# Two modulation pieces of a two-layer block, computed between the layers instead of inside the second layer's attention

## The chip, the cores and the metric

The kernel runs on one core of one Trainium2 chip. The metric is the device time of one execution in microseconds (us). TensorE is called PE below (its weight loads PEld), VectorE DVE, ScalarE ACT, and SP is the engine whose queue issues nearly all transfers from HBM.

## The reference, cut to what matters

```python
# first block: two layers (l = 0, 1) over an x stream and a context stream y, 256 rows of 1024 each
for l in range(2):
    shift, scale, gate       = split(silu(c)     @ w_mod[l] + b_mod[l], 3)   # 3 x 1024, for x
    shift_c, scale_c, gate_c = split(silu(c_ctx) @ w_mod[l] + b_mod[l], 3)   # 3 x 1024, for y
    hx = rmsnorm(x, norm_g[l]) * (1 + scale)   + shift
    hy = rmsnorm(y, norm_g[l]) * (1 + scale_c) + shift_c
    f, g, q, k, v, a = branches(h @ w_in[l], ...)        # Fourier, gated and attention branch
    ox = attend(qx, [ky; kx], [vy; vx]) * silu(ax)       # 8 heads, 256 queries, 512 keys
    x  = x + gate * (concat(fx, gx, ox) @ w_out[l])
    if l == 0:
        y = y + gate_c * (concat(fy, gy, oy) @ w_out[l])
# second block: dilated attention, convolution, gates, layer norms and a feed-forward part on x
```

Everything is float32. The product `silu(c) @ w_mod[l]` has 3072 columns per layer. The kernel computes it in six pieces of 512 columns: pieces 0 and 1 are the shift, 2 and 3 the scale, 4 and 5 the gate. A gate piece is needed only when the output projection `w_out` of its layer is added to x.

## The kernel before, in words

Four engine programs are written out by hand, one function per engine (`tensor_program`, `scalar_program`, `vector_program`, `sync_program`), and run each in its own order; semaphores join them. There is no scheduler.

**Weights.** A weight chunk is up to 128 x 1024 floats (512 KB). SP loads it into one of four raw slots (`NRAW = 4`, line 2101). ACT copies it into a rounded high part `whi` (line 960), DVE subtracts to get the low part `wlo` (line 1417), and PE multiplies three times per 128 x 128 block: high by high, high by low, low by high (lines 362, 363, 365 and 367 in `lin`, 379 to 392 in the halves `lin_first` and `lin_rest`, 409 to 415 in `lin_many`). There are five slots of high and low parts (`NHL = 5`). ACT prepares up to four chunks ahead of the one that PE uses and DVE up to three; `Weights.ahead` stops such looking ahead at a chunk that is not split. SP issues in the order in which PE takes chunks, and waits for each until the raw slot four chunks back is free: for a split chunk when DVE has made its low part, for an unsplit one when PE has read it.

**Modulation pieces.** One piece is four groups (`mod_g`, line 464). A group is one 512 KB chunk of `w_mod` and two matmuls of 128 x 32 by 128 x 512, which appear as four instructions; successive matmuls write to three different 32-row strips of one PSUM bank. After the fourth group ACT copies the bank to `modrow` (`row`, line 964), PE turns it with four transposes (`mod_t`, line 482), and DVE sums and adds the bias (`bias`, lines 1446 and 1449). Pieces of layer 0 and pieces 0 to 3 of layer 1 are computed in layer 0, with weights in places of their own. Pieces 4 and 5 of layer 1 (the gate) go through the raw slots as unsplit chunks and are computed in the second layer's attention: `mod_order(MODS1)` gives ten steps, group by group with two transposes between them, and items 0 to 9 take one each (the call `mod_step` in `for i in range(ni + 4)`).

**Attention.** An item is one head and one block of 128 queries. In item i PE does the scores of i (line 700), the transposes of i - 3 (708), the modulation step, every second item the values (723), and through item 7 one half of a gate projection `agate` (379 to 392). DVE takes the maximum (1759), ACT the exponential (1187), DVE the scaling (1766, 1768), ACT copies the transposes (1194).

**Between the layers.** PE ends layer 0 with the eight column blocks of `w_out`, then sums squares for the row norm with tiny matmuls (774 for what has been added up by DVE, 777 for the last block), DVE computes the reciprocal root (1458 to 1462), PE spreads it over the partitions (501), DVE and ACT make `hh` and `hl` of layer 1 column block by column block (1470, 983, 1480), and PE begins `lin_many`: five projections at once, as the blocks appear. Then come `lin_tm` (432 to 440), the sums 580 and 584, two transposes (592), the key, value and query projections (599, 601, 609), the Fourier branch (640, 650, 664, 665), three projections, and the transposes of the heads (619), which DVE (1682) and ACT (1114) copy out.

**PSUM.** Eight banks are handed out by `Psum.take`: of the banks not held, the one whose last use began longest ago.

Of the kernel before, what the change touches and what calls it, by code (L numbers as in the profile page):

```python
# [14 lines left out]
P = 128  # L15
# [12 lines left out]
NEG = -1.0e30  # L28
WTOTAL = 128 * (248320 - 40 * 1024)

# [174 lines left out]
def geometry(K):  # L205

    G = []
    for l in range(2):
        g = State()
        o = 0  # L210

        def area(n):
            nonlocal o
            a = K.AF[:, o:o + n]
            o += n
            return a
# [71 lines left out]

MODS0 = ((0, 4), (0, 5), (1, 2), (1, 3), (1, 0), (1, 1))
MODS1 = ((1, 4), (1, 5))  # L290


def mod_order(jobs):

    out = []
    for i, a in enumerate(jobs):
        out.append(("g", a, 0))
        if i:
            out.append(("t", jobs[i - 1], 0))
        out += [("g", a, g) for g in (1, 2, 3)]  # L300
    out.append(("t", jobs[-1], 0))
    return out

# [37 lines left out]
def tensor_program(K, e):  # L341
# [102 lines left out]
    def mod_g(l, n, g):  # L444

        key = ("mod", l, n)
        if g == 0:
            pe.wait_ge(*ps.take(key, hold=True))
        pe.wait_ge(A["c32"])
        early = l == 0 and n in EARLY  # L450
        c = None
        if early:
            pe.wait_ge(K.m_in[4 * EARLY.index(n) + g]["in"])
            w = K.early(4 * EARLY.index(n) + g).rearrange("p (k n) -> p k n", k=2)
        elif (l, n) in MODS0:
            pe.wait_ge(K.mw_in[g]["in", MODS0.index((l, n))])
            w = K.mslot(g)
        else:
            c, w, _ = weights((*key, g), ("w_mod", l, (2 * g, 2 * g + 1), (512 * n, 512)), 1024, split=False)
            w = w.rearrange("p (k n) -> p k n", k=2)  # L460
# [5 lines left out]
        if c is not None:  # L466
            W.given[c] = M.now()
        if g == 3:
            ps.drop(key)

    def mod_piece(q):

        for g in range(4):
            mod_g(*MODS0[q], g)
        if q:
            mod_t(*MODS0[q - 1])

    def mod_t(l, n):
# [4 lines left out]
        i.then_inc(*M.up(key))  # L483

    def mod_step(what, a, g):
        if what == "g":
            mod_g(*a, g)
        else:
            mod_t(*a)

# [58 lines left out]
    def layer(l):  # L549
# [181 lines left out]
        mt = lambda k: V[l, "mix", k]  # L731
        steps = mod_order(MODS1) if l else []
        half = None
        for i in range(ni + 4):
# [27 lines left out]
            if i >= ni:  # L762
                begun.append(lin_first((l, "wout", i - ni), "w_out", l, (P * (i - ni), P), 4, xh, xl, N, mt))
        for s in steps:
            mod_step(*s)
# [13 lines left out]

    layer(0)  # L780
    spread(("h", 1), TT)
    ps.drop(("h", 1, "b"))
    layer(1)


# [162 lines left out]
def scalar_program(K, e):  # L948
# [17 lines left out]

    def mod_step(what, a, g, prev):
        if what == "g":
            highs(("mod", *a, g))
            if g == 3:  # L970
                row(*a, prev)

    def square(key, src, z, n, *after):
# [44 lines left out]
    def mod_row(q):  # L1018
        row(*MODS0[q], MODS0[q - 1] if q else (0, 1))

    def layer(l):
# [179 lines left out]
        ni = len(items)  # L1201
        steps, prev = mod_order(MODS1) if l else [], (1, 1)
        for i in range(ni + 4):
# [18 lines left out]
            if l == 0 and i == 16:  # L1222
                heads_T("q", 1, 0, 1, M[l, "s", 15])
            if steps:
                s = steps.pop(0)
                mod_step(*s, prev)
                if s[0] == "g" and s[2] == 3:
                    prev = s[1]
            if i in BESIDE[l] and BESIDE[l][i][0] != "gws":
# [7 lines left out]
            if i >= ni:  # L1237
                highs((l, "wout", i - ni), 4 - i + ni)
        for s in steps:
            mod_step(*s, prev)  # L1240
            if s[0] == "g" and s[2] == 3:
                prev = s[1]

        for m in range(KD):
# [9 lines left out]
    highs((1, "fin", 1), 0)  # L1254
    ac.wait_ge(M[0, "wout", 7])
    for k in range(KD):
        make_h(1, k)
# [147 lines left out]
def vector_program(K, e):  # L1405
# [122 lines left out]
    def layer(l):  # L1528
# [26 lines left out]
        V.mark((l, "tab"))  # L1555
        if l == 0:
            bias(0, 4)

# [220 lines left out]

        ni = len(items)  # L1780
        steps = mod_order(MODS1) if l else []

        def mod_step(what, a, g_):
            if what == "t":
                bias(*a)
            else:
                lows(("mod", *a, g_))

        for i in range(ni + 4):
# [6 lines left out]
            if l == 0:  # L1796
# [26 lines left out]
                if i == 16:  # L1823
                    heads_T("q", 1, 0, 1, M[l, "s", 15])
            if steps:
                mod_step(*steps.pop(0))
            if 0 <= i - 4 and items[i - 4][1] == 7:
# [11 lines left out]
            if i >= ni:  # L1839
                lows((l, "wout", i - ni), min(3, 4 - i + ni))  # L1840
        for s in steps:
            mod_step(*s)
        for k in range(4, 8):
# [239 lines left out]
def sync_program(K, e):  # L2083
# [20 lines left out]
    def mods(q):  # L2104

        for g in range(4):
            sp.wait_ge(K.mm[("mod", *MODS0[q - 1])] if q else K.mm["mod", 0, 1])
            e.dma_start(K.mslot(g), K.wmod[16 + 4 * q + g].rearrange("p (k n) -> p k n", k=2)).then_inc(*K.mw_in[g].up(("in", q)))

# [16 lines left out]
    mods(5)  # L2126
    chunks(19, len(W.plan))
    for t in range(2):
# [6 lines left out]
def build(nc, cpack, xin, wpack, wmod, wuq, wukv, l2rows, out):  # L2135
    with ExitStack() as ctx:
# [47 lines left out]

        def mslot(g):

            G = K.G[0]
            return (G.ag[:, 0:2, :], G.ag[:, 2:4, :], G.ug, G.Pb.rearrange("p (a n) -> p a n", a=4)[:, 0:4:3, :])[g]

# [8 lines left out]
        K.m_in = [sig(f"mod_in{i}", 16) for i in range(16)]  # L2198
        K.mw_in = [sig(f"modw_in{i}", 16) for i in range(4)]
        K.c0, K.c1, K.c2, K.uq_in, K.ukv_in, K.l2_in, K.s_out = (sig(n, 16) for n in ("c0_in", "c1_in", "c2_in", "uq_in", "ukv_in", "l2_in", "out_done"))  # L2200
# [155 lines left out]
```

## Time and profile before

| what | us |
|---|---|
| median of 3 runs | 941.96 |
| lowest and highest run | 941.86, 943.33 |
| the profiled execution, its time | 940.3 |
| its span, first to last instruction | 938.5 |
| PE busy in the span | 878.3 |
| DVE busy | 615.4 |
| ACT busy | 427.1 |

The profiled execution took 1.8 us more than its span. The page gives busy times, the chain of work that ended last and the costliest groups; the timeline gives single instructions in order of time, with the idle time before them and its releaser in brackets; PEclk is the clock that TensorE was granted, 1.00 for 2.4 GHz and 0.50 for 1.2 GHz. The passage between the layers lies at about 293 to 304 us, the rest of the second layer before its attention at 304 to 378 us, and items 0 to 9 of the second layer's attention at 378 to 418 us.

### The profile page before, as it was taken

What the parts mean: (1) busy time and instruction counts of PE and PEld (TensorE: products, weight loads), DVE (VectorE), ACT (ScalarE), POOL (GpSimd) and SP (SyncE); (2) the same over time, 40 slices, a digit from 0 to 9 for tenths busy, and PEclk for the clock granted to TensorE, in tenths of its full rate; (3) what the DMA queues carried; (4) which work ended last, traced back from release to release, by engine and by line L of the source; (5) the groups of instructions that cost most, each with busy time, mean ns of one, the idle gap of its engine ahead of it and who ended that gap; (6) DMA issues with size and microseconds to landing.
All of it is one profiled execution on the core that took longest, in us unless ns stands there. A gap on an engine that the chain in (4) does not pass through costs nothing.

```text
span 938.5 us, 13733 instructions
## 1 busy us (share of the span) xinstructions
PE 878.3 (94%) x5592; PEld 724.6 (77%) x5592; DVE 615.4 (66%) x1212; ACT 427.1 (46%) x710; POOL 0.2 (0%) x4
## 2 busy tenths in 40 slices
PE   4899999999997999999999999798989799999996
PEld 1568468767685868567998888788889699999995
DVE  4432848574756579456699999986677745544555
ACT  3342426443533463555534454465543654444441
POOL 0000000000000000000000000000000000000000
PEclk9899999999998999999999999999999899999998
DMA  9674542100322213533455664442346265556551
GB/s 359 244 297 169 202 179 78 46 1 19 118 68 84 85 44 131 176 105 135 160 186 175 202 221 141 129 132 58 126 136 209 83 193 174 175 200 199 178 163 45
DMA packets 39999, 136.71 MB, mean 146 GB/s; under 512 B 4352, under 2 KB 4480, under 8 KB 39680
## 3 DMA queue, kind: packets, MB, share of 16 engines
q1 hardware_dynamic: 38928, 130.48, 41.0%
q10 hardware_dynamic: 1008, 5.36, 1.4%
q8 instruction: 44, 0.72, 0.3%
q14 instruction: 19, 0.16, 0.0%
HBM read 134.77 MB, written 1.05 MB: 145 GB/s over the span
## 4 chain that ended last, share of the span: by engine, by line
PE 80%; DVE 14%; ACT 3%; DMA 1%; issue 1%; SPq 0%; DVEq 0%; ACTq 0%
PE ps L362 9%; PE ps L363 9%; PE ps L367 8%; PE ps L922 6%; PE ps L432 3%; PE ps L434 3%; PE ps L433 3%; PE ps L464 3%; PE ps L700 3%; DVE wlo L1417 2%; DVE AF L1888 2%; PE ps L390 2%; PE ps L723 2%; PE ps L609 2%; PE ps L391 1%; PE ps L392 1%
## 5 line engine op out<-in xcount | busy, mean ns | idle before, releaser
L1417 DVE TENSOR_TENSOR wlo<-raw,whi 128x1024 fp32r<-128x1024 f32 (+2 forms) x204 | 233.8, 1161 | 59.6 <-ACT whi L960 59.4
L960 ACT ACTIVATE whi<-raw 128x1024 fp32r<-128x1024 f32 (+2 forms) x204 | 204.0, 1005 | 116.4 <-DMA raw<-wpack 51.2
L362 PE MATMUL ps<-hh,whi 128*128 128x256 f32 (+1 forms) x736 | 216.8, 295 | 3.7 <-DVE AF L1933 2.6
L363 PE MATMUL ps<-hl,whi 128*128 128x256 f32 (+1 forms) x736 | 213.1, 290 | 0.0
L367 PE MATMUL ps<-hh,wlo 128*128 128x256 f32 (+1 forms) x640 | 185.3, 289 | 0.0
L362 PEld LDWEIGHTS ps<-hh,whi 128*128 128x128 f32 x736 | 141.5, 192 | 9.7 <-issue 5.1
L363 PEld LDWEIGHTS ps<-hl,whi 128*128 128x128 f32 x736 | 141.7, 192 | 3.0 <-issue 0.7
L367 PEld LDWEIGHTS ps<-hh,wlo 128*128 128x128 f32 x640 | 123.0, 192 | 1.4
L432 PE MATMUL ps<-whi,hh 128*128 128x512 f32 (+1 forms) x192 | 70.8, 369 | 0.8 <-ACT wk L1063 0.8
L433 PE MATMUL ps<-wlo,hh 128*128 128x512 f32 (+1 forms) x192 | 70.2, 366 | 0.0
L434 PE MATMUL ps<-whi,hl 128*128 128x512 f32 (+1 forms) x192 | 70.2, 366 | 0.0
L2058 DVE TENSOR_TENSOR AF<-AF,ps 128x256 f32<-128x256 f32 x22 | 9.2, 420 | 68.7 <-PE ps L365 68.1
L1888 DVE SCALAR_TENSOR_TENSOR AF<-AF,cst 128x256 f32<-128x256 f32 x120 | 52.0, 485 | 0.4
L1759 DVE TENSOR_REDUCE AF<-ps 128x1 f32<-128x512 f32 (+1 forms) x48 | 28.7, 597 | 30.4 <-PE ps L700 30.4
L1187 ACT ACTIVATE AF<-ps,AF 128x512 f32<-128x512 f32 (+1 forms) x48 | 29.5, 615 | 33.2 <-DVE AF L1759 32.8
L700 PE MATMUL ps<-AF 96*128 96x512 f32 (+1 forms) x96 | 43.5, 535 | 0.9 <-ACT AF L1114 0.9
L1194 ACT ACTIVATE AF<-ps 128x512 f32<-128x512 f32 (+1 forms) x48 | 25.1, 523 | 38.0 <-PE ps L708 37.6
L432 PEld LDWEIGHTS ps<-whi,hh 128*128 128x128 f32 x192 | 36.0, 188 | 6.5 <-DVE wlo L1417 1.0
L464 PE MATMUL ps<-AF,c 128*32 128x512 f32 x160 | 30.1, 618 | 11.5 <-DMA AF<-wmod 11.5
L434 PEld LDWEIGHTS ps<-whi,hl 128*128 128x128 f32 x192 | 36.0, 188 | 5.6
L433 PEld LDWEIGHTS ps<-wlo,hh 128*128 128x128 f32 x192 | 36.1, 188 | 5.4
L708 PEld LDWEIGHTS ps<-cst,AF 128*128 128x128 f32 x160 | 20.2, 141 | 18.9 <-issue 13.8
(268 smaller groups left out, 1554.0 us busy)
## 6 DMA issues: line engine op xcount, KB each, us to landing
raw<-wpack SPq DMA_DIRECT2D x186, 512.0 KB, 4.2
AF<-wmod SPq DMA_DIRECT2D x40, 512.0 KB, 6.4
raw<-wpack SPq DMA_DIRECT2D x24, 256.0 KB, 3.4
XT<-xin SPq DMA_DIRECT2D x4, 512.0 KB, 5.7
raw<-wpack SPq DMA_DIRECT2D x4, 432.0 KB, 5.4
uq<-wuq ACTq DMA_DIRECT2D x2, 768.0 KB, 5.5
cst<-cpack ACTq DMA_DIRECT2D x1, 1093.0 KB, 7.9
AF<-wukv ACTq DMA_DIRECT2D x2, 512.0 KB, 6.8
```

The lines of the kernel that those rows point to most:

```text
L362: e.matmul(o, wh[:, b], xh(k), start=j == 0, stop=False, skip_group_check=True)
L363: e.matmul(o, wh[:, b], xl(k), start=False, stop=False, skip_group_check=True)
L367: e.matmul(o, wl[:, b], xh(k), start=False, stop=False, skip_group_check=True)
L432: e.matmul(o, xh(k)[:, ts], wh[:, b], start=k == 0, stop=False, skip_group_check=True)
L433: e.matmul(o, xh(k)[:, ts], wl[:, b], start=False, stop=False, skip_group_check=True)
L434: i = e.matmul(o, xl(k)[:, ts], wh[:, b], start=False, stop=k == KD - 1, skip_group_check=True)
L464: i = e.matmul(o, K.c32[:, 32 * k:32 * k + 32], w[:, j, :], start=k < 3, stop=k > 4, skip_group_check=True)
L700: e.matmul(ps.ap(key, n), g.Q[0:96, t % 2, h, :], g.K[0:96, h, 0:n], start=True, stop=True, skip_group_check=True).then_inc(*M.up(key))
L922: i = e.matmul(ps.ap(("fd", t), 512, 512 * q), y[:, f % 8, x], w[:, 512 * q:512 * q + 512], start=f == 0 and y is K.fh and w is wh, stop=f ...
L960: e.activation(W.hi(i), W.raw(i), ACT.Copy).then_inc(*HI.up(j))
L1417: e.tensor_tensor(W.lo(i), W.raw(i), W.hi(i), ALU.subtract).then_inc(*LO.up(j))
L1888: e.scalar_tensor_tensor(out=g.CV[:, m, :], in0=g.U[:, m, j:j + 256], scalar=w, in1=g.CV[:, m, :], op0=ALU.mult, op1=ALU.add).then_inc(*V. ...
```

## The change

The list `MODS` now holds pieces (1, 4) and (1, 5) as its seventh and eighth; `mod_order`, `MODS1` and the modulation steps of the attention loops are gone from PE, ACT and DVE. The weights of the two pieces no longer pass through the raw slots: `K.G[0].late`, the last 8192 columns of layer 0's area (its queries, probabilities and keys), takes them, 1024 columns a group, with four more semaphores. SP issues these eight transfers after the chunk of the last `w_out` block of layer 0, once the values of item 30 of layer 0 are done.

PE computes groups 0 and 1 of piece 4 before the sums of squares, groups 2 and 3 after them, groups 0 and 1 of piece 5 after the spreading, groups 2 and 3 after `lin_many`, followed by the transposes of piece 4; the transposes of piece 5 come after the sums of `lin_tm`. ACT copies the row of piece 4 before it makes `hh`, and the row of piece 5 after `fin(1)`. DVE adds the bias of piece 4 after the rotation tables, and that of piece 5 after the statistics.

```diff
-WTOTAL = 128 * (248320 - 40 * 1024)
+WTOTAL = 128 * (248320 - 48 * 1024)
+        g.late = K.AF[:, end - 8192:end]
-MODS0 = ((0, 4), (0, 5), (1, 2), (1, 3), (1, 0), (1, 1))
-MODS1 = ((1, 4), (1, 5))
...
+MODS = ((0, 4), (0, 5), (1, 2), (1, 3), (1, 0), (1, 1), (1, 4), (1, 5))
@@ tensor_program, mod_g
-        elif (l, n) in MODS0:
...
-            c, w, _ = weights((*key, g), ("w_mod", l, (2 * g, 2 * g + 1), (512 * n, 512)), 1024, split=False)
+            q = MODS.index((l, n))
+            pe.wait_ge(K.mw_in[g + 4 * (q == 7)]["in", q])
+            w = K.mslot(q, g)
@@ tensor_program, layer
             lin_many([spec("cq", 0), spec("cq", 1), spec("ckv", 0, True), spec("fin", 0), spec("fin", 1)], ht)
+            mod_g(1, 5, 2)
+            mod_g(1, 5, 3)
+            mod_t(1, 4)
...
         if l == 1:
+            mod_t(1, 5)
...
-            if steps:
-                mod_step(*steps.pop(0))
...
         if l == 0:
+            mod_g(1, 4, 0)
+            mod_g(1, 4, 1)
             key = ("h", 1, "s")
...
     layer(0)
+    mod_g(1, 4, 2)
+    mod_g(1, 4, 3)
     spread(("h", 1), TT)
     ps.drop(("h", 1, "b"))
+    mod_g(1, 5, 0)
+    mod_g(1, 5, 1)
     layer(1)
@@ scalar_program
-            mod_row(1)
+        mod_row(1 if l == 0 else 7)
...
     ac.wait_ge(M[0, "wout", 7])
+    mod_row(6)
@@ vector_program
-        if l == 0:
-            bias(0, 4)
+        bias(l, 4)
...
         V.mark((l, "stat"))
+        if l:
+            bias(1, 5)
@@ sync_program
-            sp.wait_ge(K.mm[("mod", *MODS0[q - 1])] if q else K.mm["mod", 0, 1])
...
+            sp.wait_ge(K.mm[("mod", *MODS[q - 1])] if 0 < q < 6 else K.mm["mod", 0, 1] if q == 0 else K.mm[0, "pv", 30])
...
-    chunks(19, len(W.plan))
+    at_out = W.of[0, "wout", 7] + 1
+    chunks(19, at_out)
+    mods(6)
+    mods(7)
+    chunks(at_out, len(W.plan))
```

PE at the passage between the layers, from the last matmul of layer 0's `w_out` to the first of `lin_many`, before. Here `128x1` rows are the sums of squares, `ps<-wk,cst` is the spreading, and four matmuls are `x4`:

```order
L365 MATMUL ps<-hh,wlo 128x512
L774 MATMUL ps<-cst,acc 128x1 x4
L777 MATMUL ps<-cst,wk 128x1 x4
L501 MATMUL ps<-wk,cst 128x512
L409 MATMUL ps<-hh,whi 128x256
```

The same place in the changed kernel:

```order
L353 MATMUL ps<-hh,wlo 128x512
L448 MATMUL ps<-AF,c32 32x512 x4
L751 MATMUL ps<-cst,acc 128x1 x4
L754 MATMUL ps<-cst,wk 128x1 x4
L448 MATMUL ps<-AF,c32 32x512 x4
L477 MATMUL ps<-wk,cst 128x512
L448 MATMUL ps<-AF,c32 32x512 x4
L397 MATMUL ps<-hh,whi 128x256
```

Three pairs of groups (`32x512 x4`, two groups each) stand between the steps of the passage; the fourth pair stands after `lin_many`.

DVE in the second layer, from the last low part before the head copies to these copies (`1682` before, `1648` now), before. `wlo` rows are low parts, `rtab` rows the rotation of the keys:

```order
L1417 TENSOR_TENSOR wlo<-raw,whi 128x1024
L1656 TENSOR_TENSOR AF<-AF 128x1536
L1637 SCALAR_TENSOR_TENSOR AF<-AF,ps 128x256
L1670 TENSOR_TENSOR AF<-AF,rtab 128x256
...
L1676 TENSOR_TENSOR AF<-AF 128x8x32
L1619 TENSOR_TENSOR AF<-AF,ps 128x256
L1637 SCALAR_TENSOR_TENSOR AF<-AF,ps 128x256
L1682 TENSOR_SCALAR AF<-ps,cst 96x4x128 x2
```

The same place in the changed kernel:

```order
L1382 TENSOR_TENSOR wlo<-raw,whi 128x1024
L1622 TENSOR_TENSOR AF<-AF 128x1536
L1603 SCALAR_TENSOR_TENSOR AF<-AF,ps 128x256
L1382 TENSOR_TENSOR wlo<-raw,whi 128x1024
L1636 TENSOR_TENSOR AF<-AF,rtab 128x256
...
L1642 TENSOR_TENSOR AF<-AF 128x8x32
L1585 TENSOR_TENSOR AF<-AF,ps 128x256
L1382 TENSOR_TENSOR wlo<-raw,whi 128x1024
L1603 SCALAR_TENSOR_TENSOR AF<-AF,ps 128x256
L1648 TENSOR_SCALAR AF<-ps,cst 96x4x128 x2
```

Two low parts, those of the gate projections `agate` 1 and 2, have moved from the attention to the stretch before the head copies, since no unsplit chunk stops the looking ahead there any more. On ACT three high parts (`agate` 1 to 3) have moved in the same way.

## Rows read from the trace of the kernel before

**Rows 1.** The chain that ended last, by engine, on the page.

```profile
PE 80%; DVE 14%; ACT 3%; DMA 1%; issue 1%; SPq 0%; DVEq 0%; ACTq 0%
```

**Rows 2.** Windows: stretch, length, busy PE, PEld, DVE, ACT, POOL, PEclk, DMA share, GB/s.

```profile
378.00:418.00 40.00, 38.06 (x240) 23.46 (x241) 19.25 (x41) 19.63 (x41) 0.00 (x0) 1.00 0.49 164
...
230.00:258.00 28.00, 25.88 (x206) 18.81 (x202) 18.74 (x37) 15.60 (x33) 0.00 (x0) 1.00 0.32 114
```

**Rows 3.** Timeline of PE in the second layer's attention: start, length, line, operation.

```profile
378.15 1.10 PE L700 MATMUL ps<-AF 96*128 96x512 f32 x2 [0.86 <-ACT AF L1114]
...
382.64 1.05 PE L464 MATMUL ps<-raw,c 128*32 128x512 f32 x4
383.62 0.39 PE L390 MATMUL ps<-hh,whi 128*128 128x256 f32 x1
...
397.75 0.50 PE L482 MATMUL ps<-cst,modrow 96*128 96x96 f32 x4
399.46 1.09 PE L723 MATMUL ps<-AF 128*64 128x128 f32 x16 [1.22 <-DVE AF L1637]
...
415.46 0.55 PE L482 MATMUL ps<-cst,modrow 96*128 96x96 f32 x4 [0.57 <-ACT modrow L964]
...
418.51 1.02 PE L700 MATMUL ps<-AF 96*128 96x512 f32 x2
```

**Rows 4.** Waits in 378 to 418 us: total, times, longest.

```profile
DVE wlo L1417 <- ACT whi L960: 16.9, 5, 5.0
...
ACT whi L960 <- DMA raw<-wpack: 8.0, 3, 3.1
```

**Rows 5.** Timeline of PE at the passage and after `lin_many`.

```profile
293.63 0.95 PE L774 MATMUL ps<-cst,acc 128*128 128x1 f32 x8
295.42 1.05 PE L777 MATMUL ps<-cst,wk 128*128 128x1 f32 x8 [0.84 <-ACT wk L976]
298.84 2.08 PE L501 MATMUL ps<-wk,cst 128*128 128x512 f32 x2 [2.37 <-DVE wk L1462]
303.55 0.55 PE L409 MATMUL ps<-hh,whi 128*128 128x256 f32 x1 [2.63 <-DVE hl L1480]
...
323.56 0.37 PE L432 MATMUL ps<-whi,hh 128*128 128x288 f32 x1 [0.85 <-ACT wk L1063]
```

**Rows 6.** Timeline of PE in the first layer: groups of a piece in a row, and a spreading.

```profile
15.66 1.90 PE L464 MATMUL ps<-AF,c 128*32 128x512 f32 x8
18.10 1.13 PE L501 MATMUL ps<-wk,cst 128*128 128x512 f32 x2 [0.53 <-DVE wk L1462]
...
104.84 2.77 PE L464 MATMUL ps<-AF,c 128*32 128x512 f32 x16
```

**Rows 7.** Windows at which the granted clock falls and rises, `lin_many`, and an early load.

```profile
297.00:298.00 1.00, 0.00 (x0) 0.00 (x0) 0.83 (x6) 0.00 (x0) 0.00 (x0) 0.81 0.00 0
307.00:308.00 1.00, 1.00 (x7) 1.00 (x7) 1.00 (x3) 0.65 (x2) 0.00 (x0) 0.57 0.00 0
304.00:321.00 17.00, 17.00 (x110) 15.93 (x110) 10.21 (x25) 5.41 (x12) 0.00 (x0) 0.89 0.01 1
50.00:60.00 10.00, 9.15 (x42) 5.90 (x43) 5.91 (x13) 7.04 (x16) 0.00 (x0) 1.00 0.87 324
```

**Rows 8.** Timeline of DVE before the attention.

```profile
343.68 0.75 DVE L1614 TENSOR_SCALAR AF<-ps,AF 128x512 f32<-128x512 f32 x1 [0.76 <-PE ps L601]
...
366.52 1.22 DVE L1417 TENSOR_TENSOR wlo<-raw,whi 128x1024 fp32r<-128x1024 f32 x1
...
373.24 4.39 DVE L1682 TENSOR_SCALAR AF<-ps,cst 96x512 f32<-96x512 f32 x6
```

**Rows 9.** Timeline: PE's last values of layer 0; ACT's high part of layer 1's first chunk.

```profile
257.11 1.09 PE L723 MATMUL ps<-AF 128*64 128x128 f32 x16
...
274.84 1.05 ACT L960 ACTIVATE whi<-raw 128x1024 fp32r<-128x1024 f32 x1
```

**Rows 10.** One line of DVE: the sum over a turned piece.

```profile
L1446 DVE TENSOR_REDUCE mod<-ps x12: 172/178/184, 19.6 to 417.6; 128x8 f32<-128x24 f32 x12
```

More of the change, by code:

```diff
@@ L287 @@
 LAST = KF - 4
-MODS0 = ((0, 4), (0, 5), (1, 2), (1, 3), (1, 0), (1, 1))
-MODS1 = ((1, 4), (1, 5))
[L293 to L302, printed above, removed]
+MODS = ((0, 4), (0, 5), (1, 2), (1, 3), (1, 0), (1, 1), (1, 4), (1, 5))
 LATE = (27, 14)
@@ L449, in mod_g @@
         pe.wait_ge(A["c32"])
-        early = l == 0 and n in EARLY
-        c = None
-        if early:
+        if l == 0 and n in EARLY:
             pe.wait_ge(K.m_in[4 * EARLY.index(n) + g]["in"])
             w = K.early(4 * EARLY.index(n) + g).rearrange("p (k n) -> p k n", k=2)
-        elif (l, n) in MODS0:
-            pe.wait_ge(K.mw_in[g]["in", MODS0.index((l, n))])
-            w = K.mslot(g)
-        else:
-            c, w, _ = weights((*key, g), ("w_mod", l, (2 * g, 2 * g + 1), (512 * n, 512)), 1024, split=False)
-            w = w.rearrange("p (k n) -> p k n", k=2)
+        else:
+            q = MODS.index((l, n))
+            pe.wait_ge(K.mw_in[g + 4 * (q == 7)]["in", q])
+            w = K.mslot(q, g)
         for j in range(2):
@@ L465, in mod_g @@
         i.then_inc(*M.up(key if g == 3 else None))
-        if c is not None:
-            W.given[c] = M.now()
         if g == 3:
@@ L473, in mod_piece @@
         for g in range(4):
-            mod_g(*MODS0[q], g)
+            mod_g(*MODS[q], g)
         if q:
-            mod_t(*MODS0[q - 1])
+            mod_t(*MODS[q - 1])
     def mod_t(l, n):
@@ L483, in mod_t @@
         i.then_inc(*M.up(key))
[L485 to L489, printed above, removed]
     def token_sums(key, nt):
@@ L731, in layer @@
         mt = lambda k: V[l, "mix", k]
-        steps = mod_order(MODS1) if l else []
         half = None
@@ L763, in layer @@
                 begun.append(lin_first((l, "wout", i - ni), "w_out", l, (P * (i - ni), P), 4, xh, xl, N, mt))
-        for s in steps:
-            mod_step(*s)
         for b in begun:
@@ L965, in row @@
         ps.give(("mod", l, n), A.now())
[L967 to L971, printed above, removed]
     def square(key, src, z, n, *after):
@@ L1018, in mod_row @@
     def mod_row(q):
-        row(*MODS0[q], MODS0[q - 1] if q else (0, 1))
+        row(*MODS[q], MODS[q - 1] if q else (0, 1))
     def layer(l):
@@ L1201, in layer @@
         ni = len(items)
-        steps, prev = mod_order(MODS1) if l else [], (1, 1)
         for i in range(ni + 4):
@@ L1223, in layer @@
                 heads_T("q", 1, 0, 1, M[l, "s", 15])
[L1224 to L1228, printed above, removed]
             if i in BESIDE[l] and BESIDE[l][i][0] != "gws":
@@ L1238, in layer @@
                 highs((l, "wout", i - ni), 4 - i + ni)
[L1239 to L1242, printed above, removed]
         for m in range(KD):
@@ L1780, in layer @@
         ni = len(items)
[L1781 to L1787, printed above, removed]
         for i in range(ni + 4):
@@ L1824, in layer @@
                     heads_T("q", 1, 0, 1, M[l, "s", 15])
-            if steps:
-                mod_step(*steps.pop(0))
             if 0 <= i - 4 and items[i - 4][1] == 7:
@@ L1840, in layer @@
                 lows((l, "wout", i - ni), min(3, 4 - i + ni))
-        for s in steps:
-            mod_step(*s)
         for k in range(4, 8):
@@ L2106, in mods @@
         for g in range(4):
-            sp.wait_ge(K.mm[("mod", *MODS0[q - 1])] if q else K.mm["mod", 0, 1])
-            e.dma_start(K.mslot(g), K.wmod[16 + 4 * q + g].rearrange("p (k n) -> p k n", k=2)).then_inc(*K.mw_in[g].up(("in", q)))
+            sp.wait_ge(K.mm[("mod", *MODS[q - 1])] if 0 < q < 6 else K.mm["mod", 0, 1] if q == 0 else K.mm[0, "pv", 30])
+            e.dma_start(K.mslot(q, g), K.wmod[16 + 4 * q + g].rearrange("p (k n) -> p k n", k=2)).then_inc(*K.mw_in[g + 4 * (q == 7)].up(("in", q)))
     piece(0)
@@ L2183, in early, with mslot @@
             return K.AF[:, i * 1024:(i + 1) * 1024]
-        def mslot(g):
+        def mslot(q, g):
             G = K.G[0]
+            if q >= 6:
+                return G.late[:, 4096 * (q - 6) + 1024 * g:4096 * (q - 6) + 1024 * g + 1024].rearrange("p (k n) -> p k n", k=2)
             return (G.ag[:, 0:2, :], G.ag[:, 2:4, :], G.ug, G.Pb.rearrange("p (a n) -> p a n", a=4)[:, 0:4:3, :])[g]
@@ L2198, in build @@
         K.m_in = [sig(f"mod_in{i}", 16) for i in range(16)]
-        K.mw_in = [sig(f"modw_in{i}", 16) for i in range(4)]
+        K.mw_in = [sig(f"modw_in{i}", 16) for i in range(8)]
         K.c0, K.c1, K.c2, K.uq_in, K.ukv_in, K.l2_in, K.s_out = (sig(n, 16) for n in ("c0_in", "c1_in", "c2_in", "uq_in", "ukv_in", "l2_in", "out_done"))
@@ L2291 @@
     wi = nc.dram_tensor("wpack", (WTOTAL,), F32, kind="ExternalInput").ap()
-    mi = nc.dram_tensor("wmod", (16 + 4 * len(MODS0), P, 1024), F32, kind="ExternalInput").ap()
+    mi = nc.dram_tensor("wmod", (16 + 4 * len(MODS), P, 1024), F32, kind="ExternalInput").ap()
     ui = nc.dram_tensor("wuq", (2, P, 1536), F32, kind="ExternalInput").ap()
@@ L2345 @@
     assert at == WTOTAL
-    pieces = [(0, n) for n in EARLY] + list(MODS0)
+    pieces = [(0, n) for n in EARLY] + list(MODS)
     wmod = np.stack([I["w_mod"][l].reshape(4, 2, P, 3 * D)[g, :, :, 512 * n:512 * n + 512].transpose(1, 0, 2).reshape(P, 1024) for l, n in pieces for g in range(4)])
```

## The prediction

> **What bounds the kernel now.** I began with the chain of the page: 80% of it is PE, 14% DVE [rows 1]. So a microsecond of PE counts where PE is not waiting, and DVE is the engine that could take over. The change touches two stretches, and their bounds differ. In 378 to 418 us, items 0 to 9 of the second layer's attention, the window has PE busy 38.06 of 40 us, DVE 19.25, ACT 19.63 [rows 2]: PE is full, and the two others have half their time free. The waits of that stretch say the same from the other side: DVE stands 16.9 us for high parts and ACT 8.0 us for raw chunks [rows 4], yet PE itself stood only 1.22 us and 0.57 us [rows 3]. At the passage between the layers it is the reverse: PE waits 0.84, 2.37 and 2.63 us in brackets, and 0.85 us after `lin_many` [rows 5]. There work on PE is free as long as it fits a gap.
>
> **The attention: removed.** One group occupies PE from 382.64 to 383.62, 0.98 us [rows 3]. Eight go: 7.84 us. Two sets of transposes go, 0.50 and 0.55 us busy, 0.92 us by the distance to what follows. The two idle times of rows 3 hang on the steps too: the one before the values came from a low part that waited for a raw chunk, the other is PE waiting for the row copy of the piece itself. With what overlaps at their edges they are 1.84 us. From the first scores at 378.15 to those of item 10 at 418.51 are 40.36 us; less 10.6 us that is 29.8 us for ten items. Is there something else that holds them at 4 us? DVE and ACT have 19.25 and 19.63 us of work for 29.8 us. The items of layer 0 with the same shapes and no modulation steps keep PE busy 25.88 of 28 us [rows 2], so 8% idle can stay. On 29.8 us that is 2.4 us. The bounds are therefore -10.6 and -8.2. I take -10.0, since the raw slots, no longer held by unsplit chunks, are just what DVE and ACT waited for.
>
> **The passage: added.** A pair of groups costs 1.90 us busy with its tail, about 1.8 us to the next start [rows 6]. Bounds: half of a whole piece in a row, 2.77 / 2 = 1.39 us [rows 6], and two lone groups, 1.96 us.
>
> First pair: it stands ahead of the sums at 293.63. The sums of the last block then start at 293.63 + 1.8 + 0.95 = 296.4 instead of 295.42: 1.0 us late, because the first gap holds only 0.84 us and lies behind the first sums [rows 5].
>
> Second pair: in the gap of 2.37 us, hidden. Third pair: in the gap of 2.63 us, hidden if the clock is full. ACT's row copy of piece 4 lies in its wait before the first `hh`.
>
> The clock: PE idled from 296.5, and in the window of 297 the granted clock fell, mean 0.81; it rose again in that of 307, mean 0.57 [rows 7]. In between the spreading took 2.08 us against 1.13 us at the full clock [rows 5, 6], and `lin_many` ran from 303.55 to 307.6 at 1.2 GHz, 4 us of which 2 would do at 2.4 GHz, since PE is busy 17.00 of 17 us there while DVE and ACT, which make its inputs, are busy 10.21 and 5.41 us [rows 7]. If the pairs keep PE busy enough, the clock stays: the spreading starts 1.0 us late and ends as before, `lin_many` starts at 303.5 and ends 2.1 us early. Behind it come the fourth pair and the transposes of piece 4, 1.8 + 0.44 us, where 0.85 + 0.25 us of waiting for ACT were; ACT's chain also starts 2.1 us earlier, so line 432 starts at about 323.0 instead of 323.56: -0.6 us. If the clock falls once and soon rises again, since PE has no long gap left, the second half of the passage costs some 1.2 us more: +0.65 us. I take 0.0 for this sum, with -0.6 and +0.65 as near ends; the far end is the first rival.
>
> The Trainium skill bears on the pairs. Rows 6 show four groups in a row in 2.77 us, 0.69 us each, against 0.98 us alone. TensorEngine Tiling (Array Packing), section Tiling Modes, lists 128 x 32 as four independent column tiles; the rule would let pieces in different strips run side by side. By it a pair of four matmuls on three strips takes two turns as does a lone pair, which agrees with 1.90 us; the sum would be the same to 0.2 us.
>
> **After `lin_many`.** The transposes of piece 5 are new on a PE that does not wait there: +0.44 us. The two biases are 0.18 us [rows 10] plus as much for the addition, four instructions, some 0.8 us on DVE with gaps. They lie ahead of the value copies, where DVE waits for PE, 0.76 us at 343.68 [rows 8]: hidden, 0; uncovered they would cost 0.8.
>
> **Moved.** The two low parts of `agate` 1 and 2 now stand before the head copies, 1.14 us each on start-to-start terms (1.22 us busy [rows 8]). Behind the last wait at 343.68 DVE runs without a gap until 373.24 + 4.39 = 377.63, and PE's first scores wait for the head copies until 378.15, where ACT's came last [rows 3, 8]. So DVE has 0.4 us of slack: 2.28 - 0.4 = 1.9 us late. The bounds are 0 (DVE catches up, since its six copies also waited for PE's transposes one by one) and 2.3. I take +1.5, nearer the upper end, as little else than the slack gives DVE time back. In the attention DVE then has these two less, where it has time.
>
> **Transfers.** The same bytes go, 4.2 MB of them earlier, behind the values that end at 258.2 us [rows 9]. At 324 GB/s, the rate of an early stretch [rows 7], they have landed by 271.2 us, 22 us before the first pair, and the first chunk of layer 1 behind them by 272.8 us, ahead of ACT's high part at 274.84 [rows 9]. Cost 0. The Trainium skill, DMA: Bandwidth & Descriptors, section Queues, rings and completion order, says that each DMA engine consumes a ring in order. This speaks against the change: by that rule the chunk can't overtake the eight transfers. With the trace's 324 GB/s it need not.
>
> **Sum.** -10.0 + 0.0 + 0.44 + 1.5 = -8.1 us. Of the profiled execution's 940.3 us that leaves 932.2 us. The median of the runs is 941.96, 1.7 us above that execution, so I forecast 933.9 us.
>
> **Rivals.**
>
> 1. The clock falls as before and stays low. For: these 32-column matmuls between tiny sums may not hold it. Against: the first layer starts with the same mix at full clock, 1.90 and 1.13 us at 15.66 and 18.10 [rows 6]. Then the second pair ends some 0.6 us after the spreading could start, the spreading takes 2.08 us, the third pair 3.6 us instead of 1.8, more than its 2.6 us gap, and `lin_many` starts 2.55 us late with no gain: 2.55 + 2.24 - 0.85 = +3.95 us in place of 0.0. Time 933.9 + 3.95 = 937.8.
>
> 2. The items are paced at the level of layer 0, and the low parts cost their full 1.9 us: -8.2 + 1.9 + 0.44 + 0.6 = -5.3, time 936.7. For: layer 0's 8%. Against: the free half of DVE and ACT.
>
> 3. Slower: the ten items keep their pace, because each waits for a chain of high part, low part, maximum and exponential that the steps on PE only filled. For: DVE's 16.9 us of waiting for high parts [rows 4]. Against: PE's idle time of under 2 us, and that what those high parts waited for were raw slots which the steps held. The price is the whole -10.0, and the added work stays: 0.65 + 0.44 + 1.5 = +2.6, time 944.6. It decides the sign if less than 2.6 us of the 10.6 are saved.
>
> 4. The weights are late. If the eight transfers ran at 114 GB/s, the mean of a stretch of the attention [rows 2], they and the chunk behind them would take 41 us and end at 299.6: the first pair would wait 2 us, and ACT would stand at its high part with the squares of `w_out` behind it. Some 8 us, which cancels the gain, time 942. Against: that stretch is low because it had little to move.
>
> **How the numbers follow.** The forecast with either near end has 0.66, rival 1 0.13, rival 2 0.13, rival 3 0.05, rival 4 0.03. Near ends of the forecast: -10.6 - 0.6 + 0.44 + 0 = -10.8 gives 931.2; -9 + 0.65 + 0.44 + 1.9 = -6.0 gives 936.0. To leave out no more than 0.2 the range takes in rivals 1 and 2, up to 939.0, and below 930.0 for another 1 us of clock. A measurement of this kernel tells 0.2%, 1.9 us, from no change. Faster by more than that: forecast, rivals 1 and 2, 0.92. Rival 4 is the same, 0.03, rival 3 slower, 0.05.
>
> **What would show it.** Items 0 to 9 take 30 to 31 us from first scores to the scores of item 10, with PE idle under 2.5 us. The second sums start about 1 us later behind the first pair. The spreading takes about 1.1 us, and no window of 0.50 stands in the first 4 us of `lin_many`; line 432's successor starts within 0.7 us of where it did. DVE's last head copy comes 1.5 to 2 us later than PE's work would ask, and the first scores name DVE as what they waited for. The prediction is wrong if the items stay near 4 us each, or if PE waits for the weights of a pair.

## The result, and the profile after

The changed kernel takes 929.89 us, the median of four runs (928.45 to 930.29), against 942.64 us for the kernel before in four runs on the same chip (941.86 to 945.23). The ratio is 0.9857, with a 95% interval from 0.9835 to 0.9880: 1.4% faster. I had forecast 933.9 us, with a range from 930.0 to 939.0: the sign was right, the gain was 4 us larger than forecast, and the time lies just below the range. The profiled execution took 929.89 us with a span of 928.1 us. That is its own median, while the profiled execution of before lay 2.3 us below the median of this comparison. This turns out to matter (last term of the account below).

Line numbers moved. Modulation groups were line 464 and are now 448, scores 700 and 680, the spreading 501 and 477, head copies 1682 and 1648, low parts 1417 and 1382, the first products of `lin_tm` 432 and 420, and the first scores of the second block 827 and 808.

The attention first, where the whole gain was expected. The window from the first scores to those of item 10 in the profile after has the columns of [rows 2]:

```profile
381.12:409.43 28.31, 28.31 (x204) 22.13 (x205) 18.19 (x37) 16.88 (x36) 0.00 (x0) 1.00 0.12 38
```

PE is busy for all 28.31 us. Before, the same items took 40.36 us [rows 3]. The other two engines have 18.19 and 16.88 us of work, so they do not set the pace. The waits of 381 to 410 us turned round:

```profile
DVE AF L1725 <- PE ps L680: 9.1, 6, 2.7
ACT AF L1169 <- PE ps L688: 7.1, 5, 2.7
```

DVE and ACT now wait for PE. Their long waits for high parts and raw chunks [rows 4] were waits for slots that the modulation chunks had held; the experiment with groups on resident data confirms it (below). The timeline of PE shows one item, from scores to scores:

```profile
383.52 1.02 PE L680 MATMUL ps<-AF 96*128 96x512 f32 x2
383.98 0.68 PE L378 MATMUL ps<-hh,whi 128*128 128x256 f32 x1
384.50 0.28 PE L379 MATMUL ps<-hl,whi 128*128 128x256 f32 x1
...
385.81 1.02 PE L680 MATMUL ps<-AF 96*128 96x512 f32 x2
```

Note the 0.46 us from the start of the scores to the start of the projection's first matmul, and the further 0.52 us to its second. Before, a group stood between the two, and more than the group went with it (below).

The passage between the layers, the same view:

```profile
295.12 1.91 PE L448 MATMUL ps<-AF,c 128*32 128x512 f32 x8
296.95 1.05 PE L751 MATMUL ps<-cst,acc 128*128 128x1 f32 x8
297.87 1.03 PE L754 MATMUL ps<-cst,wk 128*128 128x1 f32 x8
298.83 1.90 PE L448 MATMUL ps<-AF,c 128*32 128x512 f32 x8
301.26 1.13 PE L477 MATMUL ps<-wk,cst 128*128 128x512 f32 x2 [0.53 <-DVE wk L1427]
302.32 1.90 PE L448 MATMUL ps<-AF,c 128*32 128x512 f32 x8
305.02 0.35 PE L397 MATMUL ps<-hh,whi 128*128 128x256 f32 x1 [0.80 <-DVE hl L1445]
...
322.19 1.90 PE L448 MATMUL ps<-AF,c 128*32 128x512 f32 x8
324.02 0.55 PE L464 MATMUL ps<-cst,modrow 96*128 96x96 f32 x4
324.81 0.37 PE L420 MATMUL ps<-whi,hh 128*128 128x288 f32 x1 [0.24 <-ACT acc L1007]
```

This execution reached the passage 1.49 us late (295.12 against 293.63 in [rows 5]), which is no part of the change, as the first experiment shows. Less that, the second sums start 1.0 us late, `lin_many` starts where it did (305.02 - 1.49 = 303.53), and line 420 starts at 323.32 against 323.56: 0.24 us early. The spreading took 1.13 us in place of 2.08, and the window over the start of `lin_many` stands at the higher of the clock's two levels, 2.4 GHz:

```profile
305.00:309.00 4.00, 3.98 (x28) 3.74 (x29) 3.93 (x10) 2.00 (x5) 0.00 (x0) 1.00 0.02 4
```

Ahead of the attention DVE, and PE's first scores:

```profile
371.30 1.22 DVE L1382 TENSOR_TENSOR wlo<-raw,whi 128x1024 fp32r<-128x1024 f32 x1
...
375.56 1.22 DVE L1382 TENSOR_TENSOR wlo<-raw,whi 128x1024 fp32r<-128x1024 f32 x1
376.70 0.41 DVE L1603 SCALAR_TENSOR_TENSOR AF<-AF,ps 128x256 f32<-128x256 f32 x1
377.03 4.03 DVE L1648 TENSOR_SCALAR AF<-ps,cst 96x512 f32<-96x512 f32 x6
```

```profile
381.12 1.12 PE L680 MATMUL ps<-AF 96*128 96x512 f32 x2 [1.34 <-DVE AF L1648]
```

The two low parts stand ahead of the head copies, and the scores wait for DVE where they waited for ACT. From the spreading to the scores it takes 79.86 us; before it was 79.31 [rows 3, 5].

### The profile page after: what moved, and what is told of

Read it like the earlier page. It is cut to its first block, busy times and chain, and to the rows that moved or that the text cites. A ratio compares the mean times of both kernels' runs of the same rounds, so it can differ in the third digit from the quotient of the medians.

```text
span 928.1 us, 13736 instructions
## 1 busy us (share of the span) xinstructions
PE 874.2 (94%) x5592; PEld 722.0 (78%) x5592; DVE 615.1 (66%) x1212; ACT 427.3 (46%) x710; POOL 0.2 (0%) x4
## 4 chain that ended last, share of the span: by engine, by line
PE 78%; DVE 17%; ACT 2%; issue 1%; DMA 1%; SPq 0%; DVEq 0%; ACTq 0%
PE ps L350 9%; PE ps L351 9%; PE ps L355 8%; PE ps L903 6%; PE ps L420 3%; PE ps L422 3%; PE ps L421 3%; PE ps L680 3%; PE ps L448 3%; DVE wlo L1382 3%; DVE AF L1842 2%; PE ps L378 2%; PE ps L703 2%; PE ps L380 2%; PE ps L379 2%; PE ps L367 2%
## 5 line engine op out<-in xcount | busy, mean ns | idle before, releaser
L448 PE MATMUL ps<-AF,c 128*32 128x512 f32 x192 | 38.0, 617 | 11.8 <-DMA AF<-wmod 11.8
```

## The experiments

Eight runs followed, two of them repeats. The "second sequence" is the second block of the reference; its first products are the first scores of the dilated attention (line 827 before, 808 now). A span means a profiled execution; the four marks below are starts on PE in it.

| profile | spreading | first scores | item 10 | second sequence's first products | span |
|---|---|---|---|---|---|
| before | 298.84 | 378.15 | 418.51 | 589.25 | 938.5 |
| before again | 299.21 | 378.59 | 418.87 | 589.6 | 940.8 |
| after | 301.26 | 381.12 | 409.43 | 580.64 | 928.1 |
| changed again | 300.06 | 379.95 | 408.25 | 579.50 | 926.7 |

**Changed again.** The changed kernel, unchanged.

> The changed kernel once more, for the size of the effect and the spread. The changed kernel was 12.75 us faster by medians and 10.4 us by the two profiled executions. Theory: the difference between the two lies in the kernel before, whose executions differ in how often TensorE's clock falls. Then the changed kernel stays at 928 to 931 us, the kernel before at 940 to 945, a ratio of 0.986 to 0.988. Rival: the changed kernel's four executions were lucky ones; then its median here is above 931.

Measured: 929.48 us (928.54 to 930.68), ratio 0.9861 [0.9844, 0.9877]; before 942.64 in 22 runs, from 940.74 to 945.09. Items 0 to 10 take 28.30 us again. Its passage begins at 293.92, 0.3 us from before, so the 1.49 us of the first profile is spread between executions. The time stands, and the rival (a median above 931) falls.

**Before again.** The kernel before, unchanged, for a second profile.

> The kernel before, unchanged, for a second profile of it. Theory (executions of this kernel differ by a few stretches of 3.4 to 10 us at the lower clock that fall in some and not in others, and the first profile had few of them): the second has items 0 to 10 in 40.3 us again and the spread at 2.08, but other falls elsewhere, and a time of 941 to 945. Rival (the profile of before is typical): 940.3, and the falls stand where they stood.

Measured: 942.6 us in its one run, beside a median of 943.27 in 11. Items 0 to 10 take 40.28 us. The two executions of before agree to 0.5 us up to 599 us. There both wait 3.48 us; then they part. First the profile of before, then the second one, each with its window of 599 to 605 us:

```profile
599.61 0.94 PE L827 MATMUL ps<-AF 64*128 64x128 f32 x12 [3.48 <-DVE AF L1933]
607.85 0.94 PE L827 MATMUL ps<-AF 64*128 64x128 f32 x12 [0.72 <-DVE AF L1943]
```

```profile
599.00:605.00 6.00, 5.39 (x50) 5.27 (x51) 5.79 (x15) 1.92 (x4) 0.00 (x0) 1.00 0.31 90
```

```profile
599.96 1.65 PE L827 MATMUL ps<-AF 64*128 64x128 f32 x12 [3.48 <-DVE AF L1933]
609.83 0.94 PE L827 MATMUL ps<-AF 64*128 64x128 f32 x12
```

```profile
599.00:605.00 6.00, 5.04 (x28) 4.82 (x29) 5.82 (x15) 1.92 (x4) 0.00 (x0) 0.50 0.27 87
```

Behind the same wait the clock stayed at 2.4 GHz in one and stood at 1.2 GHz in the other, and the second set of products came 8.24 us behind the first against 9.87 us: 1.63 us for one fall. So my theory stands. The profile of before was one of its better executions: its mean clock was 0.979, while 20 of the 33 runs of before beside my experiments had 0.976, and the others 0.978 to 0.980. The runs of the changed kernel had 0.985 to 0.989. The Trainium skill (TensorE: Matmul & The Clock Gate, Part 1) says, of a kernel's start, that the chip's view of TensorE's activity runs freely beside the program, so that the same kernel can meet it differently from run to run. The two executions agree with that, here in the middle of a kernel.

**Groups put back, on resident data.** In the changed kernel, a group (two matmuls, four instructions) at each of eight items, whose right side is a tile that lies in SBUF all along; it takes a PSUM bank of its own for every four groups, and nothing uses the results. The diff is cut.

```diff
+STEPS = (0, 1, 2, 3, 4, 6, 7, 8)
...
+            if l and i in STEPS:
+                q = STEPS.index(i)
+                key = ("again", q // 4)
+                if q % 4 == 0:
+                    pe.wait_ge(*ps.take(key, hold=True))
+                for k in (2 * (q % 4), 2 * (q % 4) + 1):
...
+                    r = e.matmul(o, K.c32[:, 32 * k:32 * k + 32], K.XT[:, k, :], ...)
...
             if i >= 5 and i % 2:
                 values(i - 5)
```

> The changed kernel with eight dummy modulation groups put back on PE at the same items of the second layer's attention (0 to 4, 6 to 8), reading data already in SBUF and writing a bank that nobody reads: the PE work of before without its transfers, raw slots, row copies or transposes. Theory A: what left the attention is PE time, 1.17 us a group with its edges and not 0.98 (items 1 and 2 took 3.46 us before and 2.30 after). Then the dummies cost 8 x 1.17 = 9.4 us: 939.2 us, and items 0 to 9 take 37.7 us. Theory B: a group is worth 0.98 us and the rest, up to 4 us, came from the raw slots that the chunks held: 7.8 us, 937.7, items 0 to 9 in 36.1 us.

Measured: 941.26 us (939.72 to 942.46), ratio 0.9979 [0.9967, 0.9990]. Items 0 to 10 took 37.55 us, +9.24 on the 28.31 of after, 1.16 us a group: the theory's 1.17, not the 0.98 of the rival. The timeline of PE:

```profile
384.26 1.02 PE L681 MATMUL ps<-AF 96*128 96x512 f32 x2
385.22 1.05 PE L736 MATMUL ps<-XT,c 128*32 128x512 f32 x4
...
387.73 1.02 PE L681 MATMUL ps<-AF 96*128 96x512 f32 x2
```

An item takes 3.47 us, as before the change, and 2.30 after it. No transfer, slot, transpose or row copy hangs on these groups; so 9.2 of the 12.05 us that the attention lost are PE time alone. The other 2.8 us are, by subtraction, the transposes and the idle time; no run puts those back. In this run, with the pace of before but no chunks in the slots, DVE waits for PE and no longer for high parts:

```profile
DVE AF L1738 <- PE ps L681: 17.0, 9, 3.6
```

The median lies 2 us above the theory's 939.2, the profiled execution (939.8) 0.6. In that one the second sequence takes 349.0 us from its first products to the end, against 347.2 in changed again, and the clock fell there at 599 us; what the other executions had beyond it, no profile shows.

**Groups in pairs.** The same eight groups, two side by side at items 1, 3, 6 and 8; the diff is against the experiment above.

```diff
-STEPS = (0, 1, 2, 3, 4, 6, 7, 8)
+STEPS = {1: (0, 1), 3: (2, 3), 6: (4, 5), 8: (6, 7)}
```

> The changed kernel with the eight groups on resident data of the third experiment, two side by side at items 1, 3, 6 and 8 in place of one at each of eight items; what they compute is used by nothing. The third experiment put a group at 1.17 us. Theory (0.955 us is the group's own passage, as in the passage between the layers, and 0.2 is an edge between it and its wide neighbours, which two side by side share): 2.1 us a pair, items 0 to 10 in 28.3 + 8.5 = 36.8 us, and about 0.8 us below the third experiment. Rival (1.17 us is the group's own duration inside attention, edges or not): 37.7 us, the same as the third experiment.

Measured: 939.22 us (938.86 to 941.04), ratio 0.9961 [0.9948, 0.9975]; items 0 to 10 took 36.44 us, 1.11 less than with single groups, where the theory had 0.8 and the rival nothing. (The medians, from different chips, lie 2.0 us apart; the part beyond 1.11 is outside the attention.) From the scores of item 1 to those of item 2:

```profile
382.19 1.02 PE L681 MATMUL ps<-AF 96*128 96x512 f32 x2
383.14 1.91 PE L735 MATMUL ps<-XT,c 128*32 128x512 f32 x8
...
386.51 1.02 PE L681 MATMUL ps<-AF 96*128 96x512 f32 x2
```

That is 4.32 us against 2.29 of the same item after: 2.03 us a pair. Part of a group's price is an edge to its wide neighbours, which a pair pays once. TensorEngine Tiling (Array Packing) of the Trainium skill, section Tiling Modes, Key Properties, says that changing the tiling mode drains TensorE. The rows fit it: the scores overlap the following 128 x 128 matmul by 0.56 us of their 1.02, and the 128 x 32 group starts only 0.96 us behind their start.

**Six groups ahead of the last `w_out` block.** Pieces 4 and half of 5 are not spread through the passage's gaps, but stand in a row ahead of the layer's last block.

```diff
         for m in range(len(begun), KD):
+            if l == 0 and m == KD - 1:
+                for q in range(4): mod_g(1, 4, q)
+                mod_g(1, 5, 0); mod_g(1, 5, 1)
             lin((l, "wout", m), ...)
...
-            mod_g(1, 4, 0); mod_g(1, 4, 1)
...
-    mod_g(1, 4, 2); mod_g(1, 4, 3)
...
-    mod_g(1, 5, 0); mod_g(1, 5, 1)
```

> The changed kernel with the six groups of the passage moved ahead of the last block of w_out in layer 0, so that the passage has its idle gaps back; the seventh and eighth group stay behind lin_many. Theory: the gaps hid the groups and the groups kept the clock. Then the six groups cost 4.6 us in full, the clock falls at the passage as before (the spreading 2.1 us, lin_many's first 4 us at 1.2 GHz), the sums come 1 us earlier, and the kernel is about 6 us slower than the changed one: 936. Rival: the clock had nothing to do with the groups; then it stays at full here too and the kernel is 3.5 us slower, 933.4.

Measured: 938.5 us (936.74 to 941.06), ratio 0.9962 [0.9950, 0.9974]. PE, and two windows:

```profile
289.30 4.48 PE L448 MATMUL ps<-AF,c 128*32 128x512 f32 x24
...
301.09 1.05 PE L757 MATMUL ps<-cst,wk 128*128 128x1 f32 x8 [0.84 <-ACT wk L950]
304.50 2.07 PE L477 MATMUL ps<-wk,cst 128*128 128x512 f32 x2 [2.37 <-DVE wk L1426]
309.21 0.55 PE L397 MATMUL ps<-hh,whi 128*128 128x256 f32 x1 [2.63 <-DVE hl L1444]
```

```profile
303.00:304.00 1.00, 0.00 (x0) 0.00 (x0) 0.86 (x5) 0.00 (x0) 0.00 (x0) 0.50 0.00 0
...
305.00:309.00 4.00, 1.58 (x2) 0.00 (x1) 2.97 (x7) 1.70 (x4) 0.00 (x0) 0.50 0.23 66
```

With the same groups 10 us ahead of the sums, all three waits of [rows 5] are back to the hundredth, and so are the fall to 1.2 GHz and the spreading of 2.07 us. It is the pairs in the gaps that keep the clock, and not luck of one execution: in the three profiles without them (before, before again, this one) it fell at the passage, in all seven with them it did not. The time was 9.0 us above the repeat's 929.48, 3 more than the theory's 6. Of these 3, the profile has 2.6 in the second sequence, 349.8 us from its first products to the end against 347.2 in changed again; the clock fell there at 595 and 650 us, where changed again has no fall.

**Low parts given back.** Three ways to undo the 1.5 us at the first scores. First both low parts, with one each at the attention's first items:

```diff
-            lows((l, "gu", 0))
+            lows((l, "gu", 0), 2)
-            lows((l, "ggate", 1))
+            lows((l, "ggate", 1), 1)
-                lows((l, *BESIDE[l][i][:2]))
+                lows((l, *BESIDE[l][i][:2]), 1 if l and i < 8 else NHL - 2)
```

> The changed kernel with DVE's low parts of agate 1, 2 and 3 kept inside the attention (one chunk of looking ahead through item 7), so that no low part is added before the head copies. Theory: the two moved low parts cost what the first scores waited for DVE, 1.34 us in the changed kernel; the first scores then wait under 0.3 us and the kernel is 1.2 us faster than the changed one, about 928.7 against 929.9. Rival: DVE pays them back in the attention, where item 1 and 2 now wait for a low part; then the first scores come 1.2 us earlier and item 10 does not, and the time stays within 0.4 us.

Measured: 933.45 us (932.41 to 937.57), ratio 0.9911 [0.9892, 0.9931], 4 us slower than the changed kernel. The first scores came 78.54 us behind the spreading, 1.3 us sooner, as the theory had it. But items 0 to 10 took 32.33 us. PE, ACT and DVE show where:

```profile
400.78 0.63 PE L688 MATMUL ps<-cst,AF 128*128 128x128 f32 x4 [0.76 <-ACT AF L1162]
...
408.83 1.09 PE L703 MATMUL ps<-AF 128*64 128x128 f32 x16 [2.16 <-ACT AF L1169]
```

```profile
406.07 1.06 ACT L941 ACTIVATE whi<-raw 128x1024 fp32r<-128x1024 f32 x1 [4.01 <-DMA raw<-wpack]
407.04 0.58 ACT L1169 ACTIVATE AF<-ps 128x512 f32<-128x512 f32 x1
```

```profile
401.27 1.22 DVE L1382 TENSOR_TENSOR wlo<-raw,whi 128x1024 fp32r<-128x1024 f32 x1
411.28 3.49 DVE L1382 TENSOR_TENSOR wlo<-raw,whi 128x1024 fp32r<-128x1024 f32 x3
```

A low part also frees its raw slot. Done only at 401.27, it let the next chunk land so late that ACT's high part began at 406.07, behind a wait of 4.01 us; the copies and exponentials stand behind that high part on ACT, and PE's values wait for them. Three such waits, 12.2 us in all, stand in this stretch, and none in the changed kernel. The rival won, by more than it asked and through another door: not DVE's time, but the slots. So the same two low parts once more, but caught up early, one extra at item 2 and one at item 4, with the first two lines as above and the third so:

```diff
-                lows((l, *BESIDE[l][i][:2]))
+                lows((l, *BESIDE[l][i][:2]), {0: 1, 2: 2}.get(i, 3) if l else NHL - 2)
```

> The changed kernel, with the two low parts that the change made due ahead of the first scores given back to the attention, one extra at item 2 and one extra at item 4, so that never three stand in a row there (in the second experiment three did, at item 9). Theory: each of the two held the first scores up by 0.6 to 0.7 us, and the attention's items have room on VectorE for a low part of 1.22 us more each, as it waited 9.6 us for scores there; first scores 1.3 us sooner relative to the spread, items 0 to 10 in 28.3 to 28.8 us, time 928.3 to 929 (the changed kernel 929.5). Rival: VectorE has no room at any item, and each 1.22 us is paid in full; items 0 to 10 in 30.7 us, time 930.5 to 931.

Measured: 930.52 us (928.83 to 931.11), ratio 0.9859 [0.9840, 0.9877]. Spreading to scores 78.53 us, items 0 to 10 in 28.29 us: the first scores wait 0.86 us for ACT, as in the kernel before, and nothing is paid back in the attention. The time all the same missed the theory's 928.3 to 929 (see below); that it lies at the rival's 930.5 does not bear the rival out, whose 30.7 us for the items did not come. And only the later of the two, caught up at item 2:

```diff
-            lows((l, "ggate", 1))
+            lows((l, "ggate", 1), 2)
-                lows((l, *BESIDE[l][i][:2]))
+                lows((l, *BESIDE[l][i][:2]), 2 if l and i == 0 else NHL - 2)
```

> The changed kernel with only one of the two low parts (the later one) given back, and caught up at item 2. Theory: first scores 0.6 to 0.7 us sooner relative to the spread, items 0 to 10 unchanged at 28.3 to 28.6 us, time 928.8. Rival (the first of the two alone sets the hold, since the second stands beside PE's transposes): first scores no sooner, 929.5. Rival (a low part in an item is paid in full): 930.1.

Measured: 928.85 us (928.36 to 930.34), ratio 0.9849 [0.9834, 0.9864]. Spreading to scores 78.74 us, 1.12 sooner, where I had expected 0.6 to 0.7; items in 28.32 us. So the two low parts are not worth alike: giving back the later one, directly ahead of the head copies, is worth 1.1 us, and the earlier one on top of it only 0.2. With both gone DVE's six head copies take 4.38 us instead of 4.04, as in the kernel before (4.39), presumably in step with PE's transposes, and the scores wait for ACT. The earlier one alone was not given back.

In both, the 1.1 to 1.3 us don't reach the end. The wait ahead of line 350 and the window behind it, in the profile after and then in the one with both low parts caught up:

```profile
590.59 0.36 PE L350 MATMUL ps<-hh,whi 128*128 128x256 f32 x1 [2.19 <-DVE AF L1887]
```

```profile
590.00:594.00 4.00, 3.41 (x29) 3.44 (x30) 3.93 (x11) 1.93 (x4) 0.00 (x0) 1.00 0.16 37
```

```profile
590.42 0.55 PE L350 MATMUL ps<-hh,whi 128*128 128x256 f32 x1 [2.20 <-DVE AF L1887]
```

```profile
590.00:594.00 4.00, 3.58 (x17) 3.61 (x18) 3.93 (x11) 1.93 (x4) 0.00 (x0) 0.57 0.18 46
```

The same wait stands at the same time, and here the clock falls behind it; another fall follows at 641 us, which the profile after does not have either. By the medians the three versions can't be told apart, so none is shown to beat the changed kernel. Why those falls come in these profiles and not in the changed kernel's two stays open: the same wait of 2.19 to 2.20 us had no fall behind it in after, changed again and the first of these three kernels, and had one in the other two.

## Why the prediction came out as it did

What bounds: right. PE is full through the attention, 28.31 of 28.31 us, and the passage hid what was put there.

**The attention, forecast -10.0, bounds -10.6 and -8.2; measured -12.05.** This step failed: its mechanism was right and its size was not. It has three parts. The group's price was taken as 0.98 us, the distance from its start to its successor's. The successor starts sooner behind the scores once the group is gone. From scores to the projection's second matmul it was 0.95 + 0.98 + 0.22 = 2.15 us before (scores start 0.95 us ahead of the group of [rows 3], and the second matmul stood 0.22 us behind the first) and is 0.46 + 0.52 = 0.98 us after: 1.17 us a group. The experiment with single groups measured 1.16, and the one in pairs showed the edge itself. Eight times the missing 0.19 is 1.5 us. Next, I kept 0.6 us of idle time because layer 0's items have 8%: none remained. The transposes and the two waits I had right: 8 x 1.17 + 0.92 + 1.84 = 12.1. The bound of -10.6 was no bound, since it used the same 0.98.

**The passage, forecast 0.0, from -0.6 to +0.65; measured -0.24.** Each step came as written: the second sums 1.0 us late, the spreading at 1.13 us, no window of 0.50 in `lin_many`. The experiment with six groups ahead of the last `w_out` block shows the cause by taking it away.

**Transposes of piece 5, forecast +0.44; measured 0.4** (from line 420 to the first key and value products 11.65 us, before 11.25).

**Low parts, forecast +1.5; measured +1.3** on the same stretch to the first scores, so that these stand 1.5 us late in all, where the three terms made 1.9 (in the second profile of the changed kernel too: 379.95 - 378.15 less the 0.3 of its start). My reason, that little gives DVE time back, held for the later of the two, not for the earlier.

**Biases and transfers, 0.** No wait of a group for its weights stands in the rows of the passage, and nothing remained of rival 4. The eight transfers ran at 408 to 424 GB/s between 262 and 272 us in the profile after, more than 20 us ahead of the first pair.

**What the sum left out: the second sequence.** From the start of the passage to item 10 the terms make 1.5 - 12.05 = -10.55 us, and the two repeats show just that (before again, changed again: the passages begin at 293.99 and 293.92). By the first products of the second sequence 10.1 us are left of it, and by the end of the span it is 14.1. So the second sequence, for which the sum has no term, gave 4.0 us there. The fall at 598 us of before again cost 1.63 by the rows above. The one at 653 shows in the distance between two waits, first in before again, then in changed again, which has no fall there:

```profile
653.07 0.47 PE L362 MATMUL ps<-hh,whi 128*128 128x256 f32 x1 [2.62 <-DVE AF L1933]
667.42 0.39 PE L362 MATMUL ps<-hh,whi 128*128 128x256 f32 x1 [0.56 <-DVE hl L1977]
```

```profile
640.42 0.36 PE L350 MATMUL ps<-hh,whi 128*128 128x256 f32 x1 [2.62 <-DVE AF L1887]
653.26 0.39 PE L350 MATMUL ps<-hh,whi 128*128 128x256 f32 x1 [0.56 <-DVE hl L1931]
```

That is 14.35 us against 12.84, 1.51 us for the fall. The other 0.9 us have nothing to do with the clock: the waits moved. From the first to the third set of products it is 18.10 us in changed again, and 20.23 less the fall's 1.63 in before again; from there to the waits of 2.62 us it is 42.82 against 43.24. Before, PE waited 3.48 us at the second set of products; now it waits 2.2 us at line 350 and 1.26 us at the third set. The 3.48 and the 2.2 us end with the same instruction of DVE (line 1933, now 1887), the maximum over the scores, which frees their PSUM bank. The change takes and gives the banks of the two pieces at other places, and `Psum.take` then hands out others later on. The experiment with single groups on resident data fits this: it adds to the changed kernel only groups in the attention and the banks that they take, and 170 us later PE waits 0.74 and 3.48 us as before. Nothing else was run on it. Which bank is in whose way I did not follow. Between item 10 and the first products the changed kernel lost 0.5 us (a wait of 1.23 us in place of 0.74), presumably by the same shift.

**The step to the median failed too.** I had added 1.66 us for the distance of the first profile from its median, as if the changed kernel had to carry it. It did not: the profile of the changed kernel is its median, and the profile of before had been one of the better executions. Whether the change itself removes the falls at 598 and 653 us is not shown, since the low-part kernels, nearly the same programs, have falls at 590 and 641.

So of the 4.0 us by which 933.9 missed, 2.05 are the attention and 0.44 the terms ahead of it (1.94 forecast, 1.5 measured). The remaining 1.5 are, between the first two profiles, 1.8 us gained in the second sequence less the 0.5 lost ahead of it, and the 1.66 us of the median less the 1.49 us by which the changed kernel's profile came late to the passage. That the last two nearly cancel is chance.

Rival 1 (the clock stays low) fell with the row of 305 to 309 us; rival 2 (layer 0's pace) with the full PE; rival 3 (items keep their pace) with the reversed waits, and since groups on resident data gave the old pace back by PE work alone; rival 4 with the passage's rows. Rival 3 was no idle worry, though: with low parts that freed their slots late, ACT did stop PE, 2.16 us at 408.83.

## What to carry to other kernels

Cost a step that stands between two others by the distance from what is ahead of it to what is behind it, with and without it, and not by its own length: a narrow matmul group between wide ones also cost the overlap of its neighbours. Waiting gaps of PE between tiny dependent steps take such groups free and gave the clock back as well, while the same groups a little earlier gave nothing. Take a second profile of the kernel before, rather than correct a median by the distance to one profile: the distance can be clock falls that the changed kernel does not carry. And where a change takes PSUM banks at other places, look for waits that move far behind it.

## What the runs showed of the hardware

One fall of the clock behind a wait of PE cost 1.63 us, and it came in one execution and not in another of the same program behind the same 3.48 us. Another fall cost 1.51 us. Behind waits of 2.19 and 2.20 us in nearly equal programs the clock fell in two profiles and not in three. Six narrow groups in the gaps between the small steps of the passage (before: waits of 0.84, 2.37 and 2.63 us) held the clock at 2.4 GHz; in a row ahead of the last block of `w_out` they did not. A lone group of two 128 x 32 matmuls of 512 columns cost 1.16 us between wide matmuls, and 1.02 us each when two groups stood together.
